# A decoder trunk on one core: removing the matmuls without a use at TensorE's waits

## The reference, cut to what matters

```python
for i in range(DEPTH):                       # DEPTH = 2
    if i < N_A_LAYERS:
        mix = mamba2_mixer(h, ...)           # layer 0
    else:
        if i == N_A_LAYERS:
            kv = (h @ kv_w)...               # K and V, shared
        mix = dilated_attention(h, ...)      # layer 1
    h = layer_norm(DN_ALPHA * h + mix, ln_g[i, 0], ln_b[i, 0])
    ffn = hier_moe(h, ...)                   # 4 groups of 8 experts, top group, top 2 experts
    h = layer_norm(DN_ALPHA * h + ffn, ln_g[i, 1], ln_b[i, 1])
```

## Time and profile before

| | us |
|---|---|
| median of 3 runs | 1376.12 |
| lowest, highest | 1374.90, 1376.28 |
| the profiled execution | 1373.16 |
| its span, first to last instruction | 1371.3 |
| mean granted clock in it | 0.975 |

### The profile page before, as it was taken

How to read it: one execution, slowest core, us unless ns; L and a number is a source line. 1 busy time by engine, 2 the same in 40 slices (tenths; PEclk the granted TensorE clock), 3 DMA queues, 4 the chain that set the end, 5 groups by cost and what they waited for, 6 DMA issues and landing times.

```text
span 1371.3 us, 17488 instructions
## 1 busy us (share of the span) xinstructions
PE 1256.6 (92%) x6770; PEld 727.5 (53%) x6770; DVE 460.6 (34%) x963; ACT 330.9 (24%) x535; POOL 236.3 (17%) x116
## 2 busy tenths in 40 slices
PE   6998999899999999999998899998999999999994
PEld 6897777554444544444443688675444444444441
DVE  3554764422222222222222344543222222222224
ACT  4664454111111111111111545501111111111100
POOL 2464576300000000000000854320000000000002
PEclk9998999899999999999999999999999999999998
DMA  9411235859999999999998241564999999999990
GB/s 364 190 62 62 69 151 210 337 220 414 425 425 424 427 425 423 420 426 426 424 426 335 84 150 62 215 245 158 422 425 420 425 423 425 427 426 417 426 409 31
DMA packets 33812, 434.67 MB, mean 317 GB/s; under 512 B 3520, under 2 KB 5712, under 8 KB 7920
## 3 DMA queue, kind: packets, MB, share of 16 engines
q1 hardware_dynamic: 31600, 426.62, 75.2%
q10 hardware_dynamic: 1616, 5.43, 1.2%
q0 software_dynamic: 560, 2.12, 0.4%
HBM read 433.09 MB, written 1.07 MB: 317 GB/s over the span
## 4 chain that ended last, share of the span: by engine, by line
PE 43%; issue 40%; POOL 5%; DVE 4%; PEld 3%; ACT 2%; DMA 1%; PEldq 1%; POOLq 0%; SPq 0%; ACTq 0%; DVEq 0%
PE bank L587 14%; PE bank L626 7%; PE bank L576 4%; POOL split_ring L360 4%; PE bank L732 4%; PE bank L406 4%; PEld bank L533 2%; PE bank L730 2%; DVE arena L1210 1%; PE bank L641 1%; PEld bank L795 1%; PE bank L652 1%; PE bank L642 1%; DMA ring<-in_in_w 1%; POOL split_arena L287 1%
## 5 line engine op out<-in xcount | busy, mean ns | idle before, releaser
L587 PE MATMUL bank<-ring,arena 128*64 128x512 f32 x1920 | 425.2, 595 | 11.3 <-issue 11.0
L587 PEld LDWEIGHTS bank<-ring,arena 128*64 128x64 f32 x1920 | 134.8, 137 | 285.7 <-issue 285.6
L360 POOL TENSOR_TENSOR split_ring<-ring,split_ring 128x1024 fp32r<-128x1024 f32 x56 | 142.5, 2571 | 552.6 <-ACT split_ring L353 552.5
L626 PE MATMUL bank<-ring,arena 128*64 128x512 f32 x960 | 212.6, 595 | 1.7 <-DVE arena L1329 1.7
L1342 DVE TENSOR_TENSOR arena<-arena,bank 128x512 f32<-128x512 f32 x120 | 74.4, 683 | 180.0 <-PE bank L642 180.0
L626 PEld LDWEIGHTS bank<-ring,arena 128*64 128x64 f32 x960 | 66.3, 137 | 125.5 <-issue 122.1
L576 PE MATMUL bank<-arena 128*128 128x128 f32 x960 | 120.7, 280 | 2.4 <-DVE arena L1307 2.4
L576 PEld LDWEIGHTS bank<-arena 128*128 128x128 f32 x960 | 113.4, 194 | 2.5 <-issue 2.5
L1337 DVE SCALAR_TENSOR_TENSOR split_arena<-bank,arena,split_arena 128x512 fp32r<-128x512 f32 x60 | 42.3, 747 | 179.6 <-ACT split_arena L1039 179.6
L1039 ACT ACTIVATE split_arena<-bank,arena 128x512 fp32r<-128x512 f32 x60 | 38.0, 685 | 258.7 <-PE bank L626 258.7
L865 POOL TENSOR_TENSOR arena<-arena 128x1 f32<-128x1 f32 x8 | 5.2, 657 | 497.4 <-DVE arena L1266 497.4
(11 more groups left out here) (245 smaller groups left out, 1275.5 us busy)
## 6 DMA issues: line engine op xcount, KB each, us to landing
ring<-in_gate_w SPq DMA_DIRECT2D x60, 2048.0 KB, 11.8
ring<-in_up_w SPq DMA_DIRECT2D x60, 2048.0 KB, 12.2
ring<-in_down_w SPq DMA_DIRECT2D x60, 2048.0 KB, 10.8
ring<-in_in_w SPq DMA_DIRECT2D x9, 2048.0 KB, 17.1
ring<-in_out_w SPq DMA_DIRECT2D x4, 2048.0 KB, 8.8
ring<-in_kv_w SPq DMA_DIRECT2D x4, 2048.0 KB, 8.1
ring<-in_q_w SPq DMA_DIRECT2D x2, 2048.0 KB, 8.5
ring<-in_o_w SPq DMA_DIRECT2D x2, 2048.0 KB, 7.9
```

The source lines that it names most:

```text
L360: unit.tensor_tensor(split_ring[:, j % RING, here], ring[:, j % RING, here], split_ring[:, (j + 1) % RING, here], ALU.subtract).then_inc(d ...
L587: last = mm(bank[out_bank][64 * e:64 * e + 64, :], exT[:, k, 64 * e:64 * e + 64], wide(base + first + e)[:, k, :], start=k == 0, stop=k == ...
L626: last = mm(bank[5 + c][64 * e:64 * e + 64, :], hidT[:, k, 64 * e:64 * e + 64], tall(base + 4 + e)[:, k, c * 512:(c + 1) * 512], start=k = ...
```

## The change

All five calls of `keep_clock` and the function are removed, and with them the argument `idle` of `normed`. These are 17 matmuls, 34 matmul instructions in the profile, with their weight loads. The waits stay where they are and wait for the same semaphores. Nothing moves, and no other engine's stream changes.

```diff
--- before.py
+++ after.py
@@ -548,16 +548,9 @@
                 pe.drain().then_inc(mix_mm, 1)
             pe.drain().then_inc(w_used, 2)
 
-            def keep_clock(n, b):
-
-
-                for _ in range(n):
-                    mm(bank[b][:, :], ident, cst[:, C_RW:C_RW + 512], start=True, stop=True)
-
-            def normed(n, idle=(0, 0)):
+            def normed(n):
 
                 for t in range(TB):
-                    keep_clock(idle[t], 4 - t_bank(n - 1))
                     pe.wait_ge(xn_ready, (n - 1) * TB + t + 1)
                     for k in range(KD):
                         c = (k % 2) * S + t * P
@@ -652,7 +645,6 @@
                         last = mm(bank[0][:, t * 36:(t + 1) * 36], hT[:, k, t * P:(t + 1) * P], cst[:, c:c + 36],
                                   start=k == 0, stop=k == KD - 1)
                 last.then_inc(m["logit"], 1)
-                keep_clock(3, 6)
                 pe.wait_ge(m["mask"], L + 1)
                 mask = rt[:, 0:TB * E].rearrange("p (t e) -> p t e", t=TB)
 
@@ -697,7 +689,7 @@
                 expert_pair(L, base, further, before, False)
                 return further + 1
 
-            normed(1, (0, 3))
+            normed(1)
             pairs0 = experts(0, J_MOE0, None)
 
             pe.wait_ge(tb_in, 16)
@@ -778,7 +770,6 @@
                     turn(n)
                 else:
                     values(n)
-            keep_clock(5, 4)
             pe.wait_ge(att["o"], TB)
             token_transposes(pe, osb, 4, att["oT"])
             def o_block(k, tiles):
@@ -804,7 +795,7 @@
                     o_block(k, (t,))
                 pe.drain().then_inc(mix_mm, 1)
             pe.drain().then_inc(w_used, 2)
-            normed(3, (0, 3))
+            normed(3)
             experts(1, J_MOE1, pairs0)
 
         @block.gpsimd
```

## The result

| | median, us | lowest, highest | runs |
|---|---|---|---|
| before | 1373.74 | 1368.77, 1376.28 | 20 |
| after | 1377.72 | 1372.97, 1383.09 | 20 |

The changed kernel is slower: ratio 1.0036, 95% interval 1.0024 to 1.0048. The medians lie 4.0 us apart and the means 4.7. Run again beside the experiments it had 1.0029 (1.0015 to 1.0042), with 3.5 us between the medians. Because of this scatter the quotient of two medians, the quotient of two means and the ratio can differ by 0.1% and more; where they do, all are given.

The account below looks back on a forecast made before the run. The prediction took the expert loop to be bound by TensorE. Layer 0 +0.7, attention +1.2 and layer 1 +3.1 made +5.0 us on 1373.16, 1378.2, set to 1379.5 for the median; range 1375.2 to 1383.5.

Parts of the forecast that it names:

- Only three stretches matter, the loop is TensorE's: Expert loop stays at 29.69 us; only both layers' norm and router and the attention's end can change the time.
- The norms' waits give nothing back and lose clock, 0.7 us each: Norm waits, both layers: matmuls off the path; without them second transposes mostly run at 1.2 GHz, +0.7 us a layer, bounds 0 to 1.1.
- The logits are covered by GpSimd: Line 652, layer 0: logits may slow from 5.57 to 7.01 us, hidden behind GpSimd; cost 0, otherwise 1.4 us.
- The router, 0 in layer 0 and +2.4 in layer 1: Wait behind the logits: matmuls off the path; layer 1 loses the clock for ranks and gather, +2.4 us, bounds 0 to 3.8.
- The attention, -1.3 and +2.5: Attention's end: output projection starts 1.3 us earlier but loses 2.5 us at slow clock; net +1.2, bounds -3.1 to +1.8.
- the forecast's reason: Attention's end: ScalarE's first copy must follow its four line 353 operations, so line 795 starts only 1.3 us earlier.
- The sum: Layer 0 +0.7, attention +1.2, layer 1 +3.1: +5.0 us on the profiled 1373.16, giving 1378.2.
- The base: Profiled execution 2.96 us below the median 1376.12, partly a lucky clock in layer 1; forecast set between 1378.2 and 1381.1.
- the signs named: Slow second transposes, line 1374 ending with GpSimd, layer 1 low clock and slow gather, ScalarE's copy behind line 353, line 795 13 us.
- no change that can be told: Rival, whole kernel: clock already falls there with the matmuls; 1377.4 us, or 1376.0 if transposes ignore the clock; chance 0.28.
- faster: Rival, attention's end: ten instructions leave the path and little clock is lost; 1374.8 us, or 1373.0 with whole gain; chance 0.09.
- Worse: Rival: transposes leave the clock low, line 795, second transposes and both gathers slow; 9.2 us more, 1382.4; chance 0.15.

Follow-up runs that it names:

- the two parts together: Matmuls in the norms' waits and behind the router's logits removed from the kernel before, the attention's five kept: ratio 1.0026 (1.0012 to 1.0039), mean +3.6 us.
- tuned: Against before: attention's five removed, four instead of three behind the logits, one new behind the ranks, norms keep three: 0.9965 (0.9952 to 0.9977), median 1369.91 us.
- probe: Separate kernel without the model: 16 float32 matmuls of 128 columns after a burst and a wait, empty or filled; one probe took 3.7 to 3.8 or 5.2 to 6.8 us.

## Why the prediction was right, and which term was not

The eleven traces of the real kernel give the stretches of the table above more often, here norm and router, from the residual to the first gate matmul.

| in the program | norm and router, us (two stretches a trace) | mean |
|---|---|---|
| norm 3, router 3 (before; attention's removed, twice) | 30.57, 28.22, 29.97, 29.85, 29.84, 28.23 | 29.45 |
| norm 0, router 3 | 30.20, 30.71 | 30.46 |
| norm 3, router 0 | 30.34, 30.34 | 30.34 |
| norm 0, router 0 (after, again, and the two parts together) | 30.66, 32.24, 30.74, 31.95, 30.60, 30.67 | 31.14 |
| norm 3, router 3, ranks 1 (with and without the attention's) | 29.84, 28.39, 28.24, 28.24 | 28.68 |
| norm 3, router 4, ranks 1 (tuned) | 28.25, 28.22 | 28.24 |

- *Only three stretches matter, the loop is TensorE's.* Right: 29.69 us in both.
- *The norms' waits give nothing back and lose clock, 0.7 us each.* Right in its mechanism, too high for the transposes alone. With the norms' matmuls in, the second transposes took 1.09 or 1.10 us in all 14 stretches; without, 1.09 in three of eight and 1.37 to 1.97 in five, 0.36 us more on average. GpSimd's end and VectorE's copy moved by it. So "in most executions" is borne out by five of eight, none of them layer 0 of after. The whole stretch is 1.0 us longer by only two stretches (30.46 beside 29.45), and the kernel +1.9 for two norms by the means, +0.9 by the medians. What the transposes do not hold of this is in part the gather: 5.44 us in both stretches of that trace, 5.11 on average of the first row's.
- *The logits are covered by GpSimd.* Right, with 1.0 us to spare: they ended at 267.7, GpSimd at 268.7. That the copy of line 1374 ends with GpSimd whenever the logits come is not quite right. In two stretches, where the logits were early (layer 0 without the attention's matmuls, layer 1 with one behind the ranks alone), the copy was done in 0.44 and 0.56 us, a later operation of the mask chain lasted until GpSimd's end, and the ranks began 3.05 us behind it instead of 4.2.
- *The router, 0 in layer 0 and +2.4 in layer 1.* Right in the main as a sum: 0.9 us a layer by the mean stretches, 1.8 for both. Of the six stretches with all of the norms' and router's matmuls two are at 28.2 and the rest at 29.8 and more, so layer 1 of the profiled execution of before was a lucky one, as the prediction supposed. In after layer 1 paid 3.5 (0.72 and 2.79), the upper part of its bounds.
- *The attention, -1.3 and +2.5.* This step failed. The forecast was a cost of 1.2 us. In all four pairs of kernels that differ in the five matmuls alone the one without them was the faster by its mean: -1.7 and -0.9 (alone), -2.6 (with one behind the ranks), -0.4 (with norms and router removed). What was wrong is the price. From its start to the residual the output projection took 23.5 us in every trace with the five, and 24.79, 23.89, 24.61, 23.52, 24.69 and 23.55 without: +0.67 instead of +2.5. The slow start that I had from the earlier trace rows had nothing ahead of it; here sixteen transposes run in it, and their 3.4 to 3.7 us are part of it. The earlier start has the forecast's size: from the start of the product to that of the output projection 7.07 us on average of five traces with the five matmuls, 5.74 of six without, -1.33. But this is not all of the five's doing, as the next rows show. Net -0.66 by the traces.

The last matmuls of the attention, which run ahead of the five, and what ScalarE's queue did ahead of line 353; first before, then after (line 769 is now 761, 898 is 889):

```profile
...
879.57 0.64 PE L769 MATMUL bank<-arena 128*128 128x64 f32 x2
...
880.63 1.45 ACTq L898 DMA_DIRECT2D arena<-in_ln_b  x1
...
```

```profile
...
879.53 0.39 PE L761 MATMUL bank<-arena 128*128 128x64 f32 x2
...
880.34 0.45 ACTq L889 DMA_DIRECT2D arena<-in_ln_b  x1
...
```

ScalarE is idle ahead of line 353 while its queue issues this DMA. The issue took 0.45 us in six traces (0.40 us idle) and 1.35 to 2.18 in five (1.38 to 2.21 idle), and these five are the ones in which the last matmuls of the attention (line 769) took 0.63 or 0.64 us for two, at 1.2 GHz, and not 0.39. Four of them are traces with the five matmuls, one is without. Like beside like the gain is smaller or rests on one trace: with the short issue 5.92 us (one trace with the five) beside 5.66 (mean of five without), with the long one 7.36 (mean of four) beside 6.14 (one trace). So how often the five delayed the output projection, and by how much, stays open between 0.3 and 1.2 us, and that the mean came out at the forecast's 1.3 is in part luck. Nor does the forecast's reason hold in most traces: ScalarE's copy (885.55) followed line 353 directly in one of the six without the five, and in the other five it waited 0.62 us for TensorE's slow transposes.

- *The sum.* Norm and router twice (31.14 - 29.45) = +3.4, attention -0.7 to -1.3: +2.1 to +2.7. Measured were +4.0 and +3.5 by the medians, and both intervals hold only 3.3 to 5.8 us, so the stretches fall short of the whole by about 1 us, which six stretches a row can't exclude as scatter. The prediction's +5.0 had +3.8 for norm and router and +1.2 for the attention.
- *The base.* The prediction set its forecast 1.3 us above its own sum because the profiled execution lay 2.96 us below the median of three. By the median of 20 executions, 1373.74, it lay only 0.6 below. So 1376.12 was 2.4 us high, and the forecast of 1379.5, 3.4 above that median, is 5.8 above the later one, where 4.0 were measured. The rise came out close, 3.4 forecast and 4.0 measured, in part by luck: the attention's price was too high by about 2 us, and against that stood the 1.6 us taken off the sum for a lucky execution and the 1 us that the stretches don't hold. By its number the case of no change, 1377.4, was nearer; it came from the same high base and had 1.3 us of slowdown in it.

Of the signs named, three came in after: line 1365 ended with GpSimd, 931 to 940 had a clock of 0.50, and the gather of layer 1 took 6.60 us. The second transposes were over 1.5 us in layer 1 and at full clock in layer 0; ScalarE's copy did not start right behind line 353; and the 48 matmuls took 12.65 us, short of 13.

Of the rivals, "no change that can be told" is excluded by the first interval (from 0.24%; the second begins at 0.15%), and "faster" was right in that the queue at the attention outweighs the slow clock there, and too small beside the rest. "Worse" was not seen as a mean, though the slowest execution is at 1383.09.

**What stays open.** Why the issue of the DMA on ScalarE's queue takes 0.45 us in some executions and 1.35 to 2.18 in others, and whether the five matmuls have a part in it. And whether the tuned kernel owes its gain to four matmuls as a number, to the time at which the fourth ends, or to neither.

## What to carry to other kernels

A filler (a matmul whose result nothing reads) on TensorE is worth what the clock is worth to the work behind the wait, and it has to reach close to the end of the wait: three in a wait of 5 to 7 us were mostly lost, four and one more in the next gap made 2.4 us in two layers (28.24, the mean of one trace's two stretches, against 29.45). Where the wait ends at an unknown time, look whether the filler outlasts it; at the attention five did, and the kernels without them were faster by 0.4 to 2.6 us in their means. Price such things over many executions or many periods: one pair of traces here held +1.7 and -1.3 us of nothing.

## What the runs showed of the hardware

- Transposes in float32 run at the granted clock: 16 in 1.91 us at 2.4 GHz, 3.67 at 1.2. The trace of before had none slow.
- 49 of them in a row kept 2.4 GHz for the matmuls behind (278 ns a probe instruction, against 363 with nothing in the wait).
- After an idle time of 1.0 us or less the probe never ran slow (0 of 32), after 2.4 to 3.2 us in 44 of 64 cases, after 5.3 us in all 16.
- 32 matmul instructions of 36 columns in a row did not bring 2.4 GHz back: in after TensorE was busy with them from 920.18 to 927.19, the granted clock of 918 to 930 was 0.50, and so was that of 931 to 940.
- The issue of one 512 KB DMA on ScalarE's queue took 0.45 us in six traces and 1.35 to 2.18 in five.
